# Mixing beside the gathers: a two-phase encoder layer rewritten as one phase

## The reference

```python
h = rmsnorm(x, g_norm1)
z = h @ w_in
log_a = jax.nn.log_sigmoid((glr @ w_gla_a2 + b_gla_a).astype(jnp.float32)) / GLA_GATE_NORM
o_gla, S_new = gla_recurrence(gq, gk, gv, log_a, S0)
...
o_fox = fox_attention(fq, k_all, v_all, c_all, P)
...
x = x + mixed
x = x + peer(rmsnorm(x, g_norm2), w_peer_q, peer_subkeys, peer_u, peer_v)
```

## Time and profile before

| | us |
|---|---|
| median of three runs | 3622.26 (3621.23 to 3624.48) |
| profiled execution, span | 3627.2 (no other time of it is listed) |
| TensorE busy | 2778.7 (77%) |
| VectorE busy | 2582.2 (71%) |
| ScalarE busy | 1483.7 (41%) |
| POOL busy, issuing | 1316.7 (36%) |
| first gather issued | 683.5 |
| bytes moved | 1267.78 MB, mean 350 GB/s |

### The profile page before, as it was taken

The page is one execution under the profiler, slowest core; times in us unless marked ns, Lnnn a source line. Parts: engine busy times, 40 slices in busy tenths (PEclk is TensorE's granted clock), DMA queues, the critical chain, the costliest instruction groups (busy, mean ns, idle before and its releaser), DMA issues.

```text
span 3627.2 us, 32138 instructions
## 1 busy us (share of the span) xinstructions
PE 2778.7 (77%) x8313; PEld 1424.2 (39%) x8313; DVE 2582.2 (71%) x5512; ACT 1483.7 (41%) x3893; POOL 1316.7 (36%) x1154
## 2 busy tenths in 40 slices
PE   7999996677777776777787777677777777787677
PEld 3444445434333343343344343333343333343333
DVE  4333332586886768897786899878777888876786
ACT  2333333244445534444452444444524443343344
POOL 0000001234434444344444444434444543444343
PEclk9999997788888888898888898889988998888889
DMA  4010125799999999999999999999999999999998
GB/s 193 24 47 24 47 100 205 274 420 407 421 399 409 421 421 403 370 413 404 414 420 421 421 408 408 352 421 422 421 421 420 407 414 401 398 404 409 422 420 352
DMA packets 187467, 1267.78 MB, mean 350 GB/s; under 512 B 23508, under 2 KB 24492, under 8 KB 39956
## 3 DMA queue, kind: packets, MB, share of 16 engines
q0 software_dynamic: 159728, 1131.10, 76.3%
q1 hardware_dynamic: 26356, 130.32, 9.0%
q10 hardware_dynamic: 1200, 4.33, 0.3%
HBM read 1238.78 MB, written 26.88 MB: 349 GB/s over the span
## 4 chain that ended last, share of the span: by engine, by line
DMA 33%; PE 20%; DVE 15%; issue 9%; ACT 4%; POOL 2%; DVEq 0%; SPq 0%; ACTq 0%; POOLq 0%
DMA w_in<-in_peer_uv,expert_index 33%; PE ps_acc L1530 13%; DVE w_in L1701 6%; DVE v_sums L1709 3%; PE ps_scores L1506 3%; POOL w_in L1193 2%; PE ps_scores L1386 1%; ACT coef_diag L1360 1%; PE ps_scores L1474 1%; ACT gelu_u_dot_h L1355 1%; DVE key_top_index L1608 1%; DVE key_scores_rest L1609 1%; PE ps_fox_o L1404 1%; DVE key_top_index L1617 1%; DVE expert_top_index L1608 1%
## 5 line engine op out<-in xcount | busy, mean ns | idle before, releaser
L1530 PE MATMUL ps_acc<-w_in,coef_diag 128*128 128x512 f32 x2676 | 1535.2, 716 | 733.0 <-ACT coef_diag L1360 708.2
L1193 POOL DMA_INDIRECT w_in<-in_peer_uv,expert_index x1056 | 1264.7, 1198 | 1667.1 <-PE ps_acc L1530 1466.9
L1701 DVE CUSTOM_DVE_ANT_0 w_in<-w_in 128x1024 f32<-128x1024 f32 x1056 | 1285.7, 1220 | 457.6 <-DMA w_in<-in_peer_uv,expert_index 448.0
L1530 PEld LDWEIGHTS ps_acc<-w_in,coef_diag 128*128 128x128 f32 x2676 | 558.5, 223 | 1514.1 <-ACT coef_diag L1360 972.1
L1355 ACT ACTIVATE gelu_u_dot_h<-u_dot_h 128x2 f32<-128x2 f32 x528 | 107.1, 203 | 1312.7 <-DVE u_dot_h L1701 1299.5
L1709 DVE SCALAR_TENSOR_TENSOR v_sums<-w_in,coefficients,v_sums 128x1024 f32<-128x1024 f32 x387 | 495.7, 1281 | 12.7 <-ACT coefficients L1362 12.3
L460 PE MATMUL ps_z<-w_in,x_T 128*128 128x512 f32 x864 | 407.7, 622 | 6.4 <-DVE w_in L782 6.4
L1506 PE MATMUL ps_scores<-w_in,rows_T 128*128 128x256 f32 x1152 | 263.1, 382 | 0.7 <-issue 0.7
L1360 ACT ACTIVATE coef_diag<-coef_diag,gelu_u_dot_h 128x128 f32<-128x128 f32 x669 | 253.1, 398 | 17.5
L1506 PEld LDWEIGHTS ps_scores<-w_in,rows_T 128*128 128x128 f32 x1152 | 221.2, 192 | 62.7 <-issue 35.7
L460 PEld LDWEIGHTS ps_z<-w_in,x_T 128*128 128x128 f32 x864 | 165.3, 199 | 194.5 <-issue 185.1
(11 more groups left out here) (200 smaller groups left out, 2353.2 us busy)
## 6 DMA issues: line engine op xcount, KB each, us to landing
w_in<-scratch_keys_w SPq DMA_DIRECT2D x48, 1024.0 KB
w_in<-in_w_out_chunks SPq DMA_DIRECT2D x24, 1024.0 KB
w_in<-in_peer_uv,expert_index POOLq DMA_INDIRECT x1056
w_in<-in_w_in_chunks SPq DMA_DIRECT2D x6, 2048.0 KB, 25.0
w_in<-in_w_peer_q_T SPq DMA_DIRECT2D x8, 1024.0 KB, 5.9
scratch_keys_w<-w_in SPq DMA_DIRECT2D x8, 1024.0 KB, 3.9
x_T<-in_x_T POOLq DMA_DIRECT2D x9, 512.0 KB, 4.5
x_rows<-in_x_rows POOLq DMA_DIRECT2D x9, 512.0 KB, 5.2
```

The lines of the kernel that those rows point to most:

```text
L1193: pool.indirect_dma_start(out=ring[:, s % RING, :], out_offset=None, in_=dram["uv"], in_offset=bass.IndirectOffsetOnAxis(ap=idx[:, t % IDX ...
L1530: mm = pe.matmul(acc[:, c, :], diag[:, r, :], ring[:, r, D + c * 512:D + (c + 1) * 512], start=first, stop=False, skip_group_check=True)
L1701: dve.tensor_tensor_reduce(out=ring[:, s % RING, 0:D], in0=ring[:, s % RING, 0:D], in1=h2[:, t % 2, :], scale=1.0, scalar=0.0, op0=ALU.mul ...
```

## The change

`mix_phase` and `merged_phase` become one function, `stream`. Each batch now begins with `mix_front` (x is loaded; g_norm1 is multiplied into the turned rows x_T instead of w_in; the projection runs in 12 chunks of 256 columns, each 1 MB and used by the batch's tiles; gates and their sums) and `gla` (linear attention, 14 steps a tile; tile 8: 12), and goes on with `attend`, `project` and `route` as before. These steps stand in the front, so that for all batches but [0] they are written between the slots of the back. w_in is loaded once for each of the six batches instead of once. q, k, v and gated rows stay in SBUF; SP stores k, v and the gate sums as outputs, and in its queue these stores stand between the second and the third w_out chunk. The linear attention's, softmax attention's and routing's work tiles share one memory (`mixing_or_attention`). The weight chunks have two buffers instead of three; h2 has one instead of two; the descriptor scratch of POOL's transfers is set to 4096 bytes. Folding the keys is spread over the steps of tile 0's `gla` and `attend` (one unit a step). Constants are loaded on ScalarE's queue.

Two lines of the diff move most instructions: the new costs in `front_plan`. PROLOGUE goes from 78 steps to 108, all front steps from 1551 to 1810, and the rows added up by VectorE from 387 to 404 of 1056.

```diff
-WBUF = 3
+PAIRS = 6
+IN_CH = 2 * PAIRS
+CHUNKS = IN_CH + OUT_CH + PH
+WBUF = 2
...
 def front_plan():
     weight, due, on_pe = [], [], []
     for ts in BATCHES:
+        n = len(ts)
+        weight += [0.6] * (n + 1) + [3.7] * (IN_CH * n) + [0.6] * 2
+        on_pe += [True] * gla_at(ts)
+        for t in ts:
+            weight += [1.1] * gla_steps(t)
+            on_pe += [False] * gla_steps(t)
         for t in ts:
             weight += [(13.0 + 7.5 * min(t, TILES - 0.5)) / ATT_STEPS] * ATT_STEPS
...
+        def turned_rows(bi, ts):
+            if bi:
+                sp.wait_ge(s_mm, units_before(bi))
+            for i, t in enumerate(ts):
+                sp.dma_start(xT[i][:].rearrange("p k t -> p (k t)"), dram["xT"][t]).then_inc(x_in[i], 16)
...
+                    for k in range(KD):
+                        mm = pe.matmul(S[:, lo:lo + CW], xT[i][:, k, :], wb[chunk % WBUF][:, k * CW:(k + 1) * CW],
+                                       start=(k == 0), stop=(k == KD - 1), skip_group_check=True)
+                    mm.then_inc(z_mm, 1)
...
         def front():
             for bi, ts in enumerate(BATCHES):
+                yield from mix_front(bi, ts)
+                for t in ts:
+                    yield from gla(bi, t)
                 for t in ts:
                     yield from attend(t)
                 yield from project(bi, ts)
                 yield from route(bi, ts)
...
-    nc = bacc.Bacc("TRN2", target_bir_lowering=False, num_devices=1)
+    nc = bacc.Bacc("TRN2", target_bir_lowering=False, num_devices=1, dynamic_dma_scratch_size=4096)
```

More of the change, by code:

```diff
@@ new lines, in stream, with part @@
+    bT = [sb(f"b_T{i}", [P, GP, P]) for i in range(NB)]
+    ss = sb("x_sumsq", [P, NB])
+    std = sb("x_std", [P, NB])
+    rstd = sb("x_rstd", [P, NB])
+    zg = [mix[i][:, 0:512] for i in range(NB)]
+    fq = [mix[i][:, 512:] for i in range(NB)]
+    own = sb("mixing_or_attention", [P, 5440])
+    def part(at, *shape):
+        n = 1
+        for x in shape:
+            n *= x
+        names = "abc"[:len(shape)]
+        flat = own[:, at:at + n]
+        if len(shape) == 1:
+            return flat
+        return flat.rearrange(f"p ({' '.join(names)}) -> p {' '.join(names)}", **dict(zip(names, shape)))
@@ L1002, in merged_phase @@
     hrs = sb("h2_rstd", [P, ALL])
-    s1 = [sb(f"key_scores{b}", [P, 2, NKEY]) for b in range(2)]
-    s2 = sb("key_scores_rest", [P, 2, NKEY])
     kv = sb("key_top", [P, 2, TOPK])
@@ new lines, in _ @@
+            for c in range(IN_CH, IN_CH + WBUF):
+                chunk(bi, c)
+            if bi == 0:
+                sp.wait_ge(past_sp, SPLIT)
+                sp.dma_start(dram["negc_past"], past_parts[:]).then_inc(past_st, 16)
+                for x in range(2 * PH):
+                    sp.wait_ge(f_ev, 2 * (x + 1))
+                    sp.dma_start(dram["keys_w"][x // 2][:, x % 2 * D:(x % 2 + 1) * D], folded[x % 2]).then_inc(f_st[x % 2], 16)
+            stores(ts)
+            if TILES in ts and ts[0] != TILES:
+                cache()
@@ L1377, in _, with fold_keys @@
     def _(pe):
+        pe.wait_ge(init, 2)
+        pe.wait_ge(g1_in, 32)
+        def fold_keys(x):
+            if x >= FOLDS:
+                return
+            h, quarter = divmod(x, 4)
+            pe.wait_ge(wq_in[h], 16)
+            if x == 0:
+                pe.wait_ge(sub_in, 16)
+            wait(pe, f_ev, x - 1)
+            for y in range(4):
+                k, c = 2 * quarter + y // 2, y % 2
+                mm = pe.matmul(acc[:, x % 2, y * NKEY:(y + 1) * NKEY], ring[:, h, c * D + k * P:c * D + (k + 1) * P],
+                               subkeys[:, (2 * h + c) * NKEY:(2 * h + c + 1) * NKEY], start=True, stop=True)
+            mm.then_inc(f_mm, 1)
```

1551 lines of the change are left out of this document (733 added, 818 removed).

## The result

| | before | after |
|---|---|---|
| median, us | 3621.74 (3618.79 to 3624.48, 4 runs) | 3535.9 (3530.96 to 3536.71, 4 runs) |
| profiled span | 3627.2 | 3528.8 |
| first gather issued | 683.5 | 182.2 |
| gather stretch | 2920 | 3323 |
| tail behind the last gather's issue | 24 | 23 |

The ratio of the medians is 0.9755, with a 95% interval of 0.9743 to 0.9767: 2.4% faster, 86 us. The forecast was 3585, 37 us faster: the sign and the mechanism came out, the size is less than half of what was measured. 501 us went ahead of the first gather, and 403 came back behind it. This profiled execution took 3530.96 us by its own time, 2 us over its span.

A forecast was written before the change was run, and what follows sets the result against it. The kernel was taken as 684 us with few gathers, then 2920 us ruled by bytes. 200 + 2998 + 123 + 107 + 84 + 35 + 20 + 24 = 3591 us, less 5, gave 3585 us, range 3480 to 3740.

The forecast's parts named there:

- the other 20 are kept: Gather stretch: of today's 77 us over the bytes, 20 us not assigned to routing stay in the new kernel.
- Until the first gather, 200 us: Prologue: mixing of nine tiles becomes mixing of tile 0, so the first gather comes at 200 us, bounds 160 to 250.
- Bytes, 2998: Gather stretch: 1262 MB at 421 GB/s take 2998 us, 78 us more than now, if DMA were kept full.
- Routing, 123: Beside routing: fewer gathers to hide under, so VectorE rules and exceeds the bytes by 123 us together.
- Linear attention, 107: Linear attention beside gathers: VectorE with handovers takes 38 us a tile against 25 of bytes; eight tiles, 107 us.
- Softmax attention, 84: Softmax attention, denser: TensorE's 92 us against 77 of bytes, 15 over, falling to 9 for tile 1; 84 us.
- Between batches, 35: Batch starts: x_T loads only after the last routing product; 7 us lost at each of five places, 35 us.
- Less 5: End of the sum: the profiled span is 5 us over the median, so 3591 us of span becomes 3586.
- Bytes alone (3240): Rival, gather stretch: the ring of eight evens out dense stages and bytes rule alone; about 3240 us, chance 0.13.
- Lockstep: Rival, linear attention: level selects wait for TensorE, 18 us a tile on top of VectorE's 38; 3730 us, chance 0.26.
- The memory gives only its mean: Rival, gather stretch: more streams bring the rate down to 350 GB/s; 3825 us, chance 0.02.
- the rival at 358 GB/s: Gather stretch: the skill's HBM limit of about 358 GB/s for a core holds; 3744 us, the change would lose.

The follow-up runs named there:

- e5: Changed kernel, but in batches after the first each w_in chunk loads only its first eighth (outputs wrong, only time read): 3436.1 us, ratio 0.9490 to before.
- e9: Changed kernel with routing searches four steps later behind their product and the copy of the scores two steps later: 3433.8 us, ratio 0.9484 to before.
- e13: Kernel before the change, with routing searches four steps later and the copy of the scores two steps later: 3599.6 us, ratio 0.9925.
- e1: Changed kernel with VectorE adding no rows of v beside routing and linear attention, TensorE adding 108 more: 3461.1 us, ratio 0.9532 to before.
- e7: Changed kernel with only the planner's cost of a linear attention step raised from 1.1 to 2.2: 3510.7 us, ratio 0.9698 to before.
- e11: The e10 kernel with the later searches of e9 as well: 3320.9 us, ratio 0.9174 to before.
- e10: Changed kernel with e1's rows on TensorE, one more VectorE wait and planner costs rebalanced further, softmax attention's included: 3381.9 us, ratio 0.9330 to before.

## Why the prediction was right or wrong, point by point

The mechanism came out: the work ahead of the first gather came back behind it as bytes and as dense stages. What failed is the size, 37 us forecast and 86 measured, and most of all one kind of term: time in which DMA stands still between stages, "7 us lost at each of five places: 35" and "the other 20 are kept". The rows show DMA nearly full at the batches' starts, and the stages there are not above their bytes.

**What bounds the kernel.** Right: 2920 us of bytes became 3323 us in which bytes rule the projections (e5), the out-projections (422 GB/s) and softmax attention of tiles 4 and 5 (412 GB/s from 1561 to 1720 us), and not the rest. 1262 MB was right within 2 MB (380 GB/s x 3323 us = 1263 MB), and so is the price of a block: 421 to 422 GB/s in the quiet stretches of both kernels.

**Until the first gather, 200 us: measured 182.** TensorE's records give the parts: projection done at 81 us (80 forecast), linear attention at 106 (25 us for 40), softmax attention at 138 (32 for 36), then 44 to the first gather (44). They are read off these starts (us, length), the first product of linear attention, of softmax attention, the turn of its result, and the out-projection:

```profile
81.69 0.66 PE L1077 MATMUL ps_scores<-ident,z_gla_qk 128*128 128x128 f32 x4 [0.78 <-ACT mix_rows L772]
...
105.62 0.60 PE L1163 MATMUL ps_turn<-ident,fox_k 128*128 128x128 f32 x4
...
137.89 1.97 PE L1196 MATMUL ps_turn<-ident,mix_rows 128*128 128x128 f32 x8 [0.85 <-DVE mix_rows L1496]
...
140.59 9.24 PE L1218 MATMUL ps_scores<-weight_chunk,rows_T 128*128 128x256 f32 x32 [0.73 <-issue]
```

The step that failed is "with table loads and handovers I take 40": alone on the engines, linear attention ran in little more than VectorE's 22 us. In the records, folding's products (L1002, about 1.1 us a unit) stand in TensorE's gaps between the levels.

**Bytes, 2998: right.** The blocks of the table by stage make 3005 us.

**Routing, 123: measured 177.** VectorE's busy time was right, 227 forecast and 232.0 measured for tiles 4 and 5; the 28 us of waits came as 34. Over their bytes, tiles 4 and 5 stand 52 us (41 forecast), tiles 2 and 3 57 (41), tiles 6 and 7 27 (15), and the rest makes up the 177. The step that failed is the size of these excesses, as VectorE's waits and idle time beside its work came out longer than the 28 us taken along. Of these waits the one for key scores could be had away in this kernel (e9), while it had cost little in the kernel before (e13).

**Linear attention, 107: measured 116.** VectorE's work was right: 34 us a tile forecast, 67.6 us for tiles 6 and 7 together. What the sum booked for handovers, 4 us a tile, came as 8 there (84 us less 67.6, for two tiles). e1 took some 15 rows, 19 us of VectorE's work, off these stages and they got 17 us shorter, so its work is in the chain though it is busy only 0.80 of the time. But the stage isn't held by that work alone: e7 put 63 gathers more there for 96 us, 1.5 us each, less than their bytes. That the rest is handovers fits this; no run took one handover out.

**Softmax attention, 84: measured 58.** The step that failed is "64 + 16 x 1.8 = 92 us of TensorE", carried over to the other tiles as an excess that falls from 15 us to 9. It gave the right size for tile 7 (122 us with 44 gathers, 121 by the sum). The excess runs the other way: 26 and 19 us for tiles 1 and 2, near nothing for tiles 4, 5 and 6. The sum came as near as it did by luck.

**Between batches, 35, and "the other 20 are kept": next to nothing.** This is the larger part of the miss. The projection stages lie 16 us under their bytes, the out-projection 12 under. In the 30 us around the starts of the five batches the rate was 364, 380, 407, 416 and 415 GB/s, which at 421 GB/s is 9 us lost in all, 7 of them at the first two. The rows of the first two and of the fourth:

```profile
269.00:299.00 30.00, 22.92 (x83) 14.89 (x84) 26.33 (x52) 15.12 (x40) 11.92 (x10) 0.89 0.94 364
607.00:637.00 30.00, 18.56 (x59) 11.06 (x60) 27.41 (x61) 15.69 (x41) 10.41 (x7) 0.77 0.94 380
...
2048.00:2078.00 30.00, 19.91 (x53) 12.05 (x52) 27.94 (x53) 15.22 (x40) 11.39 (x9) 0.70 1.01 416
```

TensorE waited 19.7 us in all for w_in chunks, 11.3 of them ahead of the first gather. A gap on one queue was taken for a gap in the stretch. That the ring of eight and the two chunks loaded ahead bridge it fits these rows; no run changed the ring. For the 20 that were kept no row shows a place either.

**"Less 5".** The offset between span and median was taken over from the kernel before. Here the median stands 7 us above the profiled span (its own time 2 above, the runs' spread the rest): 12 us in the wrong direction.

So of the 50 us between the sum, 3586, and 3536: 18 from the prologue, 44 from the stretch and 1 from the tail, less the 12 of the offset. In the stretch 83 us were too much for batch starts, kept loss and stages that lie under their bytes, 26 for softmax attention; 63 were too little for routing and linear attention. The sum had the right total within 2% by luck in part, because its errors went both ways.

**The signs named ahead.** First gather near 200 (182), 375 GB/s over 3365 us (380 over 3323), VectorE at 0.88 beside routing (0.87), low DMA stretches there and dips at linear attention (0.91, 0.86), 421 GB/s beside the projection (401 to 406).

**The rivals.** Bytes alone (3240): not yet, but it is where the kernel goes: e11 stands 80 us above it. Lockstep (3730, from 4.6 us a tile on): the selects' waits for TensorE were 8.5 and 7.1 us in the whole run, under 2 a tile:

```profile
  PE ps_turn L1089: 8.5, 3
  PE ps_scores L1089: 7.1, 5
```

Nor is it the few gathers there that keep this wait short: in e7, with 63 gathers more beside linear attention, the same selects waited 5.1 us in the whole run, and in e10, with 80 more, 9.7.

"The memory gives only its mean" (3825): out, with 410 GB/s over 2920 us in the kernel before and 406 GB/s over 3115 us in e11. The same rows put the rival at 358 GB/s out. The Trainium skill (Perfetto Trace Analysis, Engine Utilization, Roofline) says that 358 GB/s is a core's share when both cores of a pair are at work, and that a single active core may draw more, up to about 435 GB/s through its 16 DMA engines. The rows agree: 420 to 422 GB/s where DMA is full.

## What to carry to other kernels

A stage is priced by busy work **and** by the waits of the engine that works most there; when a change thins out the traffic above a wait, the wait can come due at its full length, so look first at the waits that bytes have hidden. What a wait is worth depends on what else fills its stage: a us of the same wait was worth 0.39 us in the kernel before, about 1 with the change, and 0.5 or 0.2 after the plans had brought DMA back to 0.98 of the gather stretch. When work moves from a phase of its own beside other work, set the density anew, stage by stage, from rows at the new place: three numbers of the planner were worth 97 us, more than the 86 of the rewrite itself. And don't book a gap at each seam while a ring of buffers lies across it.
